# High and low parts of the first attention's gated output on GpSimd instead of VectorE

## What is computed

```python
def mixer_a(h, hc, w_in, sinks, w_o, cos, sin, ctx_out):
    """Windowed GQA with per-head sink; latent queries also read all context keys."""
    q, k, v, g = jnp.split(h @ w_in, [...], axis=-1)
    ...
    y = (o * jax.nn.silu(g)) @ w_o
    ...
    yc = (oc * jax.nn.silu(gc)) @ w_o
```

## Time and profile before

| | us |
|---|---|
| Time, median of 3 runs | 2364.59 |
| lowest and highest | 2364.46, 2369.76 |
| the profiled execution's own time | 2363.17 |
| its span | 2361.4 |
| TensorE busy | 2183.5 (92%) |
| VectorE busy | 1072.2 (45%) |
| ScalarE busy | 842.9 (36%) |
| GpSimd busy | 689.8 (29%) |

### The profile page before, as it was taken

How to read it: one execution, slowest core, us unless ns; L and a number is a source line. 1 busy time by engine, 2 the same in 40 slices (tenths; PEclk the granted TensorE clock), 3 DMA queues, 4 the chain that set the end, 5 groups by cost and what they waited for, 6 DMA issues and landing times. The chain is left out here.

```text
span 2361.4 us, 29756 instructions
## 1 busy us (share of the span) xinstructions
PE 2183.5 (92%) x11442; PEld 1677.8 (71%) x11442; DVE 1072.2 (45%) x1782; ACT 842.9 (36%) x1563; POOL 689.8 (29%) x383
## 2 busy tenths in 40 slices
PE   5999888899999998997898999998998788999997
PEld 3888555688555544885876888886985566788886
DVE  2421888523355523636616625243117724725253
ACT  3322655323444423335123323223116633322231
POOL 1221000243000002330142444444443343444443
PEclk8999999899999999998689999998999899999999
DMA  7221332132000012320022333322231122333332
GB/s 267 63 63 54 92 97 82 45 108 63 18 1 1 1 36 72 90 81 1 28 63 58 104 101 89 104 82 80 90 89 32 32 65 69 99 97 91 98 94 67
DMA packets 255889, 169.16 MB, mean 72 GB/s; under 512 B 5776, under 2 KB 247159, under 8 KB 254599
## 3 DMA queue, kind: packets, MB, share of 16 engines
q1 hardware_dynamic: 251792, 157.31, 22.4%
q0 software_dynamic: 2336, 8.97, 1.2%
q10 hardware_dynamic: 1623, 0.98, 0.1%
HBM read 165.10 MB, written 2.14 MB: 71 GB/s over the span
## 5 line engine op out<-in xcount | busy, mean ns | idle before, releaser
L1260 POOL TENSOR_TENSOR WL<-raww,WH 128x1024 fp32r<-128x1024 f32 (+1 forms) x239 | 564.7, 2368 | 982.7 <-ACT WH L309 865.6
L354 PE MATMUL ps<-HH,WH 128*128 128x512 f32 (+1 forms) x1368 | 526.2, 385 | 37.2 <-DVE HL L475 19.6
L355 PE MATMUL ps<-HL,WH 128*128 128x512 f32 (+1 forms) x1368 | 521.8, 381 | 0.0
L356 PE MATMUL ps<-HH,WL 128*128 128x512 f32 (+1 forms) x1368 | 520.9, 381 | 0.0
L309 ACT ACTIVATE WH<-raww 128x1024 fp32r<-128x1024 f32 (+1 forms) x239 | 244.9, 1034 | 328.4 <-PE ps L356 328.3
L354 PEld LDWEIGHTS ps<-HH,WH 128*128 128x128 f32 x1368 | 261.7, 191 | 97.8 <-issue 24.5
L356 PEld LDWEIGHTS ps<-HH,WL 128*128 128x128 f32 x1368 | 261.1, 191 | 49.5
L355 PEld LDWEIGHTS ps<-HL,WH 128*128 128x128 f32 x1368 | 261.4, 191 | 47.1
L557 ACT ACTIVATE PB<-ps,NB 128x256 f32<-128x256 f32 (+5 forms) x256 | 167.9, 656 | 101.3 <-DVE NB L546 64.1
L604 PE MATMUL ps<-ident,PB 128*128 128x128 f32 x952 | 156.7, 281 | 23.1 <-DVE PT L622 16.1
L542 DVE TENSOR_REDUCE NB<-ps 128x1 f32<-128x768 f32 (+4 forms) x128 | 92.5, 723 | 128.5 <-PE ps L532 127.5
(11 more groups left out here) (296 smaller groups left out, 3318.3 us busy)
## 6 DMA issues: line engine op xcount, KB each, us to landing
raww<-in_ffn_w_up SPq DMA_DIRECT2D x88, 512.0 KB, 3.8
raww<-in_ada_w SPq DMA_DIRECT2D x32, 512.0 KB, 3.6
raww<-in_ffn_w_down SPq DMA_DIRECT2D x32, 448.0 KB, 3.7
raww<-in_odd_w_in SPq DMA_DIRECT2D x24, 512.0 KB, 3.7
raww<-in_even_w_in SPq DMA_DIRECT2D x21, 512.0 KB, 3.8
raww<-in_a_w_in SPq DMA_DIRECT2D x20, 512.0 KB, 3.8
raww<-in_ffn_w_down SPq DMA_DIRECT2D x16, 512.0 KB, 3.8
ADA<-in_ada_w SPq DMA_DIRECT2D x6, 1024.0 KB, 18.0
```

The lines of the kernel that those rows point to most:

```text
L354: nc.tensor.matmul(out, lh, rh, start=start and k == ks[0], stop=False)
L355: nc.tensor.matmul(out, lh, rl, start=False, stop=False)
L356: ins = nc.tensor.matmul(out, ll, rh, start=False, stop=stop and k == ks[-1])
L1260: nc.gpsimd.tensor_tensor(lo, raw_slot(k), hi.bitcast(F32), ALU.subtract).then_inc(*split_lo.mark(k))
```

## The change

The cast and the subtraction of 14 of the 16 outputs go from VectorE to GpSimd. VectorE's `a_keep` now ends after the product when m is below 7, and marks it in `dve_out` as "a scaled". A new function `a_parts_pool` makes the high and the low part on GpSimd; `att_pool` calls it at the pair's step in `keep_at`, behind the gate of that step. It waits for VectorE's product, then for each of its own two results. `att_pool` also waits for its own gate product. TensorE's next claim of bank 7 waits for "a scaled" instead of `o_made`, and the output projection waits for GpSimd's low part. The two pairs of m = 7 stay on VectorE as before.

```diff
--- before.py
+++ after.py
@@ -627,7 +627,7 @@
 
             n = len(A["jobs"][r]["pv"])
             if q0 == 0:
-                claim(pe, 7, (o_made, (A["name"], A["jobs"][r]["pair"])))
+                claim(pe, 7, A["kept"](A["jobs"][r]["pair"]) if "kept" in A else (o_made, (A["name"], A["jobs"][r]["pair"])))
                 for h in (r - 1, r):
                     for i in range(A["jobs"][h]["nq"]):
                         for g, (first, blks, eng) in enumerate(A["jobs"][h]["tiles"][i]["lots"]):
@@ -699,6 +699,9 @@
                     pool.wait_ge(*bc_made[A["name"], q])
                     nc.gpsimd.tensor_tensor(g, g, A["bc"][:, 0:g.shape[-1]], ALU.mult)\
                         .then_inc(*gated.mark(A["name"], q))
+                    pool.wait_ge(*gated[A["name"], q])
+                if "parts_pool" in A and t in A["keep_at"]:
+                    A["parts_pool"](pool, A["jobs"][A["keep_at"][t]])
 
 
         def pair_q_high(act, A, m, hh):
@@ -909,8 +912,25 @@
             r0, nr = (0, S) if seg == "lat" else (S, C)
             g = a_gate(job)
             dve.wait_ge(*gated["A", r])
+            if m < 7:
+                nc.vector.tensor_tensor(g, ps[:, 7, 0:nr], g, ALU.mult).then_inc(*dve_out.mark("a scaled", m, seg))
+                return
             chain(dve, dve_step, nc.vector.tensor_tensor(g, ps[:, 7, 0:nr], g, ALU.mult))
             two_parts(dve, a_oh[:, m, r0:r0 + nr], a_ol[:, m, r0:r0 + nr], g, ("A", (m, seg)))
+
+        def a_parts_pool(pool, job):
+
+            m, seg = job["pair"]
+            if m == 7:
+                return
+            r0, nr = (0, S) if seg == "lat" else (S, C)
+            g = a_gate(job)
+            pool.wait_ge(*dve_out["a scaled", m, seg])
+            nc.gpsimd.tensor_copy(a_oh[:, m, r0:r0 + nr], g).then_inc(*pool_out.mark("a high", m, seg))
+            pool.wait_ge(*pool_out["a high", m, seg])
+            nc.gpsimd.tensor_tensor(a_ol[:, m, r0:r0 + nr], g, a_oh[:, m, r0:r0 + nr].bitcast(F32), ALU.subtract)\
+                .then_inc(*pool_out.mark("a low", m, seg))
+            pool.wait_ge(*pool_out["a low", m, seg])
 
         fill_at = {int(2.6 * f): f for f in range(len(fillers) + 1)}
 
@@ -965,7 +985,8 @@
                     ins = nc.vector.tensor_tensor(MROW[:, :], MROW[:, :], bank(key)[:, 0:256], ALU.add)
                 ins.then_inc(*dve_out.mark("mrow", r))
 
-        ATT_A = pair_prep(finish_att({"name": "A", "jobs": a_jobs(), "scale": HD ** -0.5, "keep_o": a_keep,
+        ATT_A = pair_prep(finish_att({"name": "A", "jobs": a_jobs(), "scale": HD ** -0.5, "keep_o": a_keep, "parts_pool": a_parts_pool,
+                                      "kept": lambda p: (dve_out, ("a scaled",) + p) if p[0] < 7 else (o_made, ("A", p)),
                                       "fill_pe": a_fill_pe, "fill_dve": a_fill_dve, "per": 4, "gate": a_gate,
                                       "pt": lambda r: ((0, 0), (2, 0), (1, 0), (1, C))[r % 4],
                                       "pt_free": lambda r: (r - 4) | 1,
@@ -1422,7 +1443,7 @@
             att_pe(pe, ATT_A)
             for m in range(8):
                 lin(pe, "ao", ("a_o", m), m, lambda r0, nr: lambda k: (a_oh[:, k, r0:r0 + nr], a_ol[:, k, r0:r0 + nr]),
-                    BOTH, lambda m, s: (x_made, ("ao", m, s)), ready=(lambda k: o_made["A", (k, "ctx")]) if m == 0 else None)
+                    BOTH, lambda m, s: (x_made, ("ao", m, s)), ready=(lambda k: pool_out["a low", k, "ctx"] if k < 7 else o_made["A", (k, "ctx")]) if m == 0 else None)
 
         def mixer_b_pe(pe):
```

## The result

| | before | changed | ratio [95%] |
|---|---|---|---|
| first comparison, median | 2364.53 us (4 runs) | 2346.06 us (4 runs, 2342.98 to 2347.94) | 0.9919 [0.9903, 0.9935] |
| first repeat | 2364.82 us (29 runs) | 2348.60 us (6 runs, 2341.41 to 2352.28) | 0.9934 [0.9919, 0.9949] |
| second repeat | 2361.68 us (11 runs) | 2347.03 us (6 runs, 2339.75 to 2349.26) | 0.9924 [0.9901, 0.9946] |
| profiled execution of the first comparison | 2363.17 us (span 2361.4) | 2342.98 us (span 2341.2) | |

The change makes the kernel 0.7 to 0.8% faster: 18.5, 16.2 and 14.7 us by the three pairs of medians. The forecast was 2352.3 us, 12.3 us less. Its direction and its place were right, its size was too small: the first median lies 0.9 us under the lower end of the range, those of the repeats inside it.

What follows compares the result with a forecast made beforehand. TensorE, busy 92%, was taken as the bound, waiting 15.6 us for VectorE's copies in the first attention. Lat 8.35 plus ctx 2.68 and 1.29 made 12.3 us; 2364.6 - 12.3 = 2352.3 us, range 2347 to 2359.5.

Steps and rivals of the forecast that it cites:

- What bounds the stage: First attention: TensorE and VectorE hold it in turn, GpSimd idle 92%; TensorE's transposes wait 15.6 us for VectorE's copies.
- the rule of the smaller value: First attention, each output: the gain is the smaller of TensorE's stall behind it and the VectorE time removed.
- Step 1: First attention: VectorE loses two instructions in each of 14 outputs, 15.3 us, of which 12.3 us shorten the path.
- Step 2: First attention: GpSimd gains 28 instructions, 24 us with waits, covered by its idle time, no time on the path.
- Step 3: Added waits in the first attention delay nothing; TensorE's earlier claim of bank 7 is worth 0, a 2.0 us wait stays.
- Rival A: First attention: something else, such as scores or exponentials, is late next and half the gain returns; 2358.5 us, chance 0.20.
- B: First attention: all VectorE time removed counts, 15.3 us, even where the stall is smaller; 2349.3 us, chance 0.14.
- C: First attention: GpSimd's work locks VectorE out, L546 first, and makes it slower; 2373 us, chance 0.04.
- D: Stages after the first attention: the 12 us shift is lost there, by lower clock or a transfer; 2363 us, chance 0.04.

Runs made afterwards that it cites:

- experiment 3: Against the kernel before, only the seven ctx outputs' high and low parts moved to GpSimd: 2360.13 us, ratio 0.9986.
- experiment 1: Both kernels run again without edit: the kernel before 2364.10 us, ratio 1.0004; the changed kernel 2348.60 us, and a third time 2347.03 us.
- experiment 5: Against the changed kernel, TensorE's next claim of bank 7 waits for GpSimd's low part instead of VectorE's product: 2356.43 us, ratio 0.9964.

## Why the prediction was right in kind and too small in size

- **What bounds the stage: right.** The two engines hold it in turn. Taking VectorE's 28 instructions took the stalls with them, and the fifth lat output, with a stall of only 0.32 us behind it, gained least (0.61 us), as the rule of the smaller value wanted, though twice what it said. (That GpSimd stands idle 92% of the time holds for the first period; over the 214 us of the earlier trace rows it is 89%.)
- **Step 1, the term that failed.** I compared the start of the same TensorE instruction in both traces at each output. The lat outputs gained 1.54, 0.96, 1.54, 1.63, 0.61, 1.55 and 1.63 us, 9.46 where the sum had 8.35; the ctx ones 0.76, 0.80, 0.79, 0.76, 0.79, 0.76 and 0.79, 5.45 where it had 3.97. Three things were mis-sized, and a fourth was left out:
  1. *The listed stall is shorter than the time lost.* It counts from the modelled end of the matmul before. In the trace of before one transpose group follows unstalled and one stalled:

```profile
255.88 0.23 PE L532 MATMUL ps<-maskb,identb 128*128 128x128 bf16 x1
255.94 0.72 PE L604 MATMUL ps<-ident,PB 128*128 128x128 f32 x5
...
257.85 0.23 PE L532 MATMUL ps<-maskb,identb 128*128 128x128 bf16 x1
259.45 0.41 PE L604 MATMUL ps<-ident,PB 128*128 128x128 f32 x2 [1.38 <-DVE PT L622]
```

     From start to start 0.06 and 1.60 us: the stall cost 1.54, not 1.38. That is 0.16 in each of the periods 1, 3 and 6, and 0.09 in the second. In the fifth 0.29 of the 0.61 us were in no listed stall at all: the group of transposes ahead of the stall of 0.32 ran 1.06 us before and 0.72 after.

```profile
364.98 1.06 PE L604 MATMUL ps<-ident,PB 128*128 128x128 f32 x5
```
```profile
356.59 0.72 PE L604 MATMUL ps<-ident,PB 128*128 128x128 f32 x5
```

  2. *VectorE lost more than the two instructions.* I counted from the cast's start (1.51 and 0.67 us). But the cast had itself waited for the product's completion, and what follows the product now doesn't: 0.59 against 0.72 us for lat (256.64 - 256.05; 256.41 - 255.69), 0.34 against 0.45 for ctx (264.10 - 263.76; 265.43 - 264.98). Removed are 1.64 and 0.79 us, which is what the outputs with long stalls gained.
  3. *Periods 1, 4 and 6 of the ctx outputs.* I let only the stall of 0.43 count. The stall behind it shrank too, from 0.71 to 0.54 us:

```profile
267.89 0.44 PE L604 MATMUL ps<-ident,PB 128*128 128x128 f32 x2 [0.71 <-DVE PT L622]
```
```profile
265.88 0.33 PE L604 MATMUL ps<-ident,PB 128*128 128x128 f32 x1 [0.54 <-DVE PT L622]
```

     With item 1 that makes 0.76 instead of 0.43. My reason for letting only 0.43 count, that the copy reads what TensorE transposes after the stall, was wrong in part.
  4. *The clock.* 1.55 us came back because the stretch of lower clock in the seventh period (experiment 3) was gone. In the earlier trace rows it is hidden in the stage's mean of 0.97.

  The account: 12.3, 1.1 more in the lat outputs, 1.5 more in the ctx ones and 1.55 of clock, less the 0.5 and 0.35 us at the end, is 15.6 us, against 15.5 from the traces. With 15.5 us the first median would have been about 2349.0, inside the range. The other 3.0 us of that comparison's 18.5 are scatter between executions, so that the first median fell outside was chance on top of the mis-sized term; both repeats' medians, 2348.60 and 2347.03, lie inside.
- **Step 2, GpSimd at no cost: right, and shown.** The parts took 0.61 and 1.28 us (lat), 0.40 and 0.73 (ctx): 7 x 3.02 = 21.1 us, the page's difference. Leaving them out and lengthening them left the periods as they were. The Trainium skill (GPSIMD Engine Reference, section 4.1 Engine selection) would have put this work on VectorE; its ratio of about two holds here, 1.28 us against 0.69 for the lat low part, and was no loss, since GpSimd was idle.
- **Step 3, the early claim at 0: right of the kernel before, wrong of the change.** While VectorE made the low part, TensorE did not wait for it. On GpSimd it ends 3.86 us after the product's start (259.91 - 256.05) instead of 2.30 (257.99 - 255.69), and then the old claim would cost 8.1 us. I priced this edit on its own, where it had to be priced together with step 2. The forecast itself wasn't hurt, as the change makes both edits. The waits that the change adds were not all free either: that of GpSimd for its own last gate product costs the 0.35 us ahead of the projection.
- **Rival A** (half returns): didn't come. Stalls with another releaser are small, the largest in the seven periods a single one of 1.08 us behind L719, and a stall of that length stood at the same place before (379.19). **B** (all VectorE time counts, 15.3 us) came nearer in its number, and the periods of 24.5 us on average that I had named as its sign are what was measured. Its mechanism is nearly what happened in 12 of the 14 outputs: all ctx ones gained the whole 0.76 to 0.80 us and five lat ones 1.54 to 1.63 of 1.64. The lat outputs of periods 2 and 5 gained 0.96 and 0.61 us only, and there the rule of the smaller value was needed. In all, TensorE gained 14.9 of the 17.0 us that VectorE lost, by the intervals of item 2. **C**: tested and fallen. L546 ran in 212 to 216 ns all 128 times. By the Trainium skill (SBUF — State Buffer, section SBUF: two separate sides) an instruction with two SBUF inputs or in a two-port mode is shut out while the other engine holds the ports. For L546 the runs show no such hold. They do show it again where I had seen it, in the changed kernel's last high part:

```profile
429.13 7.54 DVE L903 CAST a_oh<-ARENA 128x256 fp32r<-128x256 f32 x1
```
```profile
429.49 7.02 POOL L1281 TENSOR_TENSOR WL<-raww,WH 128x1024 fp32r<-128x1024 f32 x3
```

  The cast ends 0.16 us behind the last of these three products. But its record starts 0.36 us ahead of the first, while GpSimd still has its transfer of 428.86 to 429.47, and alone it takes 0.29: what held it from the start isn't shown.

  **D** (lost in later stages): nothing was lost there, by experiment 1.

## What to carry to other kernels

Price a removed wait by the starts of the instructions on both sides of the stall, against the same pair where nothing stalls, and price a removed chain from the product ahead of it to what now follows that product: the two shortcuts taken here made the 14.9 us that the outputs gained look like 12.3. When work goes to a slower idle engine, look at once at everyone who waits for its result: here half of the gain hung on claiming the bank at the product instead of at the low part. And read a difference of a few us between two whole profiles only after cutting them into stages, since the part that the change doesn't touch moved by up to 11 us between profiles.

## What the hardware did that I had not expected

- A stall of 1.8 us can be followed by a stretch of about 3.4 us at a granted clock of 0.50, which added 1.55 us. It did so in the seventh period each of three times, and behind a wait of 1.41 us in experiment 5. But a stall of that length right ahead is not needed: the repeat of before has a stretch in its first period, from about 269.7 on, and the stalls of the 5 us ahead of it are 0.43, 0.71 and 0.26 us, with one of 1.38 us 9 us ahead. The same stalls had full clock behind them in the first profile. The repeat, then the first profile:

```profile
270.00:273.00 3.00, 3.00 (x20) 2.40 (x14) 2.22 (x7) 2.40 (x6) 0.00 (x0) 0.52 0.54 131
```
```profile
270.00:273.00 3.00, 2.54 (x27) 1.82 (x26) 2.87 (x8) 1.57 (x5) 0.00 (x0) 1.00 0.62 175
```

  And a stall of 1.79 us at 340.42 in the kernel before was followed by full clock:

```profile
340.00:344.00 4.00, 3.58 (x29) 1.91 (x30) 3.06 (x8) 2.41 (x7) 0.00 (x0) 1.00 0.21 35
```

  What makes the difference stays open; I made no run for it.
- The same program took from 1909.0 to 1916.5 us behind the loop in three profiles, and over both kernels and the variants from 1908.3 to 1919.2. In the three compared above the granted clock of one 120 us window, 0.72 or 0.79, goes with it. What sets it from one execution to the next is open too.
- Four GpSimd casts in a row (2.65 us) beside VectorE's maximum, bias and copy changed no period by more than 0.2 us (171.36 us for the seven, 171.35 without any of GpSimd's parts): VectorE's instructions that read PSUM, and the 128x1 one from SBUF, were held by none of them here.
